# Hybrid attention/LRU layer: attention work placed between the matmul groups of two projections, with a new order of weight tiles

## The reference

```
mod = silu(cond) @ w_mod + b_mod            # 24 blocks of 512 columns: shift, scale, gate twice
h   = rmsnorm(x) * (1 + scale) + shift
u   = h @ w_in                              # 2048 x 5120, split into heads of four mixers
A: differential attention, 4 heads, two softmaxes per head, p0 - lam * p1, then rmsnorm
B: RG-LRU: conv of width 4, gates, scans in both directions, times gelu(gate)   (512 wide)
C: neighbourhood attention, 4 heads, with a bias table
D: grouped attention, 4 query heads, 2 key heads, rms-normed and rotated q and k
y   = concat(A, B, C, D) @ w_out            # 2048 x 2048
x   = x + gate * norm(y)
x   = x + gate2 * norm(swiglu(modulate(norm(x)) @ w_ffn_in) @ w_ffn_out)   # hidden 5632
```

## Time and profile before

| | |
|---|---|
| median of 3 runs | 1934.77 us (1931.64 to 1935.92) |
| profiled execution, its own time | 1931.91 us |
| its span | 1930.1 us |
| PE busy | 1801.7 us, 93% |
| DVE, ACT, POOL busy | 859.8, 653.1, 156.3 us |
| input projection starts at PE | 53.06 us |
| last input matmul to first output-projection matmul group after the turns of A | 513.6 to 641.0 us |
| output projection | 641.0 to about 782.9 us |
| tail to first `up` matmul | to 797.97 us |
| up and down projections | to about 1908 us |

### The profile page before, as it was taken

One profiled execution on the slowest core, in us unless ns is written; L12 is line 12 of the kernel. 1 busy time (PEld: TensorE's weight loads), 2 busy tenths in 40 slices (PEclk: granted clock), 3 DMA queues, 4 the chain that ended last, 5 costly groups with the idle time before them and its releaser, 6 DMA issues.

```text
span 1930.1 us, 22007 instructions
## 1 busy us (share of the span) xinstructions
PE 1801.7 (93%) x9291; PEld 1526.0 (79%) x9291; DVE 859.8 (45%) x1197; ACT 653.1 (34%) x915; POOL 156.3 (8%) x223
## 2 busy tenths in 40 slices
PE   4999979999876899799999999999999999999995
PEld 0666646667555688799999999999999888888884
DVE  4355457722176333743333333333333345555553
ACT  2322234422265233432222222222222234444441
POOL 1000285520010000200000000000000000000000
PEclk9999989999989899899999999999999999999998
DMA  9677755797810333143333333333333333333321
GB/s 374 266 307 300 293 229 217 283 321 302 332 72 1 131 111 129 45 152 131 129 116 127 132 131 129 116 127 131 131 129 116 126 109 131 131 124 119 128 88 66
DMA packets 46298, 315.20 MB, mean 163 GB/s; under 512 B 5388, under 2 KB 7816, under 8 KB 8888
## 3 DMA queue, kind: packets, MB, share of 16 engines
q1 hardware_dynamic: 43328, 298.99, 41.4%
q0 software_dynamic: 2544, 11.59, 1.6%
q10 hardware_dynamic: 328, 3.21, 0.4%
HBM read 308.40 MB, written 5.37 MB: 163 GB/s over the span
## 4 chain that ended last, share of the span: by engine, by line
PE 85%; DVE 5%; POOL 3%; DMA 3%; ACT 2%; issue 1%; DVEq 0%; SPq 0%; ACTq 0%; POOLq 0%
PE ps L867 38%; PE ps L617 8%; PE ps L618 8%; PE ps L619 8%; PE ps L659 5%; PE ps L660 5%; PE ps L661 5%; PE ps L596 3%; DMA raw<-in_weights 2%; DVE wlo L928 1%; POOL pool_t L1322 1%; DVE smalls L1146 1%; DMA ident<-in_ident_c 1%; PE ps L841 1%; PE ps L790 1%
## 5 line engine op out<-in xcount | busy, mean ns | idle before, releaser
L928 DVE TENSOR_TENSOR wlo<-raw,whi 128x1024 fp32r<-128x1024 f32 x376 | 459.7, 1234 | 872.7 <-ACT whi L323 872.5
L323 ACT ACTIVATE whi<-raw 128x1024 fp32r<-128x1024 f32 x376 | 392.8, 1059 | 938.3 <-PE ps L867 505.4
L867 PE MATMUL ps<-h_hi,whi 128*128 128x384 f32 x1408 | 471.3, 335 | 0.1
L867 PE MATMUL ps<-h_hi,wlo 128*128 128x384 f32 x1408 | 470.3, 334 | 0.0
L867 PE MATMUL ps<-h_lo,whi 128*128 128x384 f32 x1408 | 470.3, 334 | 0.0
L867 PEld LDWEIGHTS ps<-h_hi,whi 128*128 128x128 f32 x1408 | 264.3, 188 | 0.2 <-issue 0.2
L867 PEld LDWEIGHTS ps<-h_lo,whi 128*128 128x128 f32 x1408 | 264.3, 188 | 0.0
L867 PEld LDWEIGHTS ps<-h_hi,wlo 128*128 128x128 f32 x1408 | 264.3, 188 | 0.0
L617 PE MATMUL ps<-whi,j_hi 128*128 128x512 f32 x528 | 209.8, 397 | 4.6 <-DVE j_lo L1267 4.6
L659 PE MATMUL ps<-whi,h_hi 128*128 128x512 f32 x480 | 195.6, 407 | 17.7 <-ACT U L350 10.7
L618 PE MATMUL ps<-whi,j_lo 128*128 128x512 f32 x528 | 206.5, 391 | 0.0
(11 more groups left out here) (238 smaller groups left out, 1518.3 us busy)
## 6 DMA issues: line engine op xcount, KB each, us to landing
raw<-in_weights SPq DMA_DIRECT2D x284, 1024.0 KB, 4.9
xT<-in_x_t ACTq DMA_DIRECT2D x1, 3072.0 KB, 13.0
out<-x_sb POOLq DMA_DIRECT2D x3, 1024.0 KB, 4.7
x_sb<-in_x_sample POOLq DMA_DIRECT2D x1, 2048.0 KB, 10.3
gw<-in_lru_gate_w SPq DMA_DIRECT2D x4, 256.0 KB, 2.9
out<-U POOLq DMA_DIRECT2D x4, 256.0 KB, 8.1
nabias<-rpb_pad POOLq DMA_DIRECT2D x16, 64.0 KB, 12.5
x_sb<-in_x_prompt POOLq DMA_DIRECT2D x1, 1024.0 KB, 6.0
```

The source lines that it names most:

```text
L323: nc.scalar.activation(whi[:, 2 * (g % RING) + b], raw[:, t % RAW, HK * b:HK * b + HK].rearrange("p k n -> p (k n)"), ACT.Copy).then_inc(w ...
L867: return nc.tensor.matmul(ps[bank][:, 0:T], w[:, k % KH * P:(k % KH + 1) * P], xs[:, k, :], start=first, stop=last)
L928: V.tensor_tensor(wlo[:, 2 * (t % RAW) + b], raw[:, t % RAW, HK * b:HK * b + HK].rearrange("p k n -> p (k n)"), whi[:, 2 * (g % RING) + b] ...
```

## The change

Attention is cut into tasks and these are set into gaps. Step s now has three gaps, one after each token block's 12 matmuls; gap g = 3s + block. The output projection's 16 tiles become steps 40 to 55. Tasks are K and Q (turn keys, queries), S (scores), P (transpose probabilities), V (value product). A table gives each gap its tasks: D heads from gap 85, A heads from 107, C heads from 131 to 152; 69 gaps hold something, 142 bursts in all. All outputs are now stored row-wise in U and turned back by three transposes per head (`turn_back`), D's in gaps 120 to 123, A's in 138 to 141, C's in 143 to 153. The output projection goes K part by K part (B, D, A, C), each step a sum of its own that ACT copies (first part) or DVE adds to `y1` (`group_add`). Division by the softmax sum moves behind the value product (`evict`). The squares of D's norm move from POOL to ACT (`norm_squares`), the LRU's tanh from `lru_in` into `lru_gates`, the loads of the caches to other places, and the first `in` tile is read as the ninth tile, before the four tiles of row 2 of `mod`. In the tail all three token blocks are done behind the last `group_add`, with the residual add in four pieces of 512.

```
-IN_BLOCKS = [3, 4, 8, 9, 0, 1, 2, 5, 6, 7]
+IN_BLOCKS = [3, 8, 4, 9, 0, 1, 2, 5, 6, 7]
+OUT_KG = [1, 3, 0, 2]
+STEPS = IN_STEPS + OUT_N * KG
+def mod_tiles(s):
+    if s < IN_STEPS:
+        m, first = 2 + s // 2, s % 2 * 2
+        return m, [] if s == 0 else [0, 1, 2, 3] if s == 1 else [first, first + 1]
+    if s - IN_STEPS in (2, 3, 4, 5):
+        m, first = 22 + (s - IN_STEPS - 2) // 2, s % 2 * 2
+        return m, [first, first + 1]
+    return 0, []
```

The places of a head's tasks, from its first gap, for A and for the others:

```
+            s_at, p_at, v_at, q_at, span = (0, 2, 4), (2, 4, 6), (3, 5, 7), 3, 6
...
+            s_at, p_at, v_at, q_at, span = (0, 1, 3), (2, 3, 5), (3, 4, 6), 4, 5
```

PE, behind each token block of a step, and the wait before each turn, since all turns share one bank:

```
+                    if tb == 0 and mid is not None and s >= EARLY * KG:
+                        mod_turn(mid)
+                    gap(TB * s + tb)
...
+            def t_bank(task):
+
+                if T_NO[task]:
+                    pe.wait_ge(t_cp, T_NO[task])
+                else:
+                    pe.wait_ge(l_tanh, 16)
```

ACT, per step:

```
+                if s > EARLY * KG:
+                    gap(s - 1, 2)
+                if KG - 1 in kgs:
+                    rows_out(m)
+                hi(*step_key(s + 1))
...
+                if s >= EARLY * KG:
+                    gap(s, 0)
+                    gap(s, 1)
```

DVE, per step (n is 0 to 3 in the last four steps), and the tail:

```
+                if s > EARLY * KG:
+                    gap(s - 1, 2)
+                if n >= 0:
+                    diagonal(G_M, n, 1, 2 * n)
+                lo(*step_key(s + 1))
+                if n > 0:
+                    for tb in range(TB):
+                        y1_gate(n - 1, tb)
...
+                if s >= EARLY * KG:
+                    gap(s, 0)
+                    if n >= 0:
+                        diagonal(G_M, n, 0, 2 * n + 1)
+                    if KG - 1 in kgs:
+                        mod_out(m)
...
+                if s >= EARLY * KG:
+                    gap(s, 1)
+            gap(STEPS - 1, 2)
             dve.wait_ge(x1_in, 32)
             for tb in range(TB):
+                y1_gate(3, tb)
                 dve.wait_ge(y_g, 9 + tb + 1)
                 dve.wait_ge(rs_done, 2 + tb)
-                V.scalar_tensor_tensor(x_sb[:, tb, :], y1[:, tb, :], yrs[:, tb:tb + 1], x_sb[:, tb, :],
-                                       ALU.mult, ALU.add).then_inc(x1_ok, 1)
+                for n in range(4):
+                    x = x_sb[:, tb, n * NC:n * NC + NC]
+                    ins = V.scalar_tensor_tensor(x, y1[n][:, tb, :], yrs[:, tb:tb + 1], x, ALU.mult, ALU.add)
+                ins.then_inc(x1_ok, 1)
```

POOL (the 16 bias loads follow the load of kvC, as before):

```
+            pool.dma_start(kvD[:, :, :], cgqa.rearrange("b a j p h d -> p (b a j) (h d)")).then_inc(kvd_in, 16)
...
+            pool.wait_ge(l_y, 4)
+            pool.dma_start(kvA[:, :, :], cdiff.rearrange("b a j p h d -> p (b a j) (h d)")).then_inc(kva_in, 16)
...
+            pool.wait_ge(pv_ps, A0)
+            pool.wait_ge(l_xp, 4)
+            pool.wait_ge(stored, stores[0])
             pool.wait_ge(rpb_w, 80)
+            pool.dma_start(kvC[:, :, :], cna.rearrange("b a j p h d -> p (b a j) (h d)")).then_inc(kvc_in, 16)
```

More of the change, by code:

```diff
@@ L66, in tile_plan @@
     for s in range(STEPS):
[L67 to L70, removed]
+        m, kgs = mod_tiles(s)
+        plan += [("mod", m, kg) for kg in kgs] + [step_key(s)]
     plan += [("up", f, part) for f in range(FK) for part in range(2)]
@@ L272, in mod_bank @@
         def mod_bank(m):
[L274 removed]
+            return 7 if m < 8 and m % 2 else 3
         def last_step(n):
@@ new lines, in queries_turn, with scores @@
+            def queries_turn(hd):
+                t_bank(("Q", hd))
+                for tb in range(TB):
+                    ins = nc.tensor.transpose(ps[6][:, tb * P:(tb + 1) * P], q_of(TB * hd + tb), ident[:, :])
+                ins.then_inc(t_ps, 1)
+            def scores(u):
+                kind, h, tb = UNITS[u]
+                hd = u // TB
+                pe.wait_ge(t_cp, T_NO["Q", hd] + 1)
+                if kind == "A" or u == C0:
+                    pe.wait_ge(ex, u)
+                elif u >= 2:
+                    pe.wait_ge(ex, u - 1)
+                for j in range(nsoft(kind)):
+                    part = slice(64 * j, 64 * j + 64) if kind == "A" else slice(0, P)
+                    ins = nc.tensor.matmul(ps[score_bank(u, j)][:, 0:width(tb)], qT[hd % 2][part, tb * P:(tb + 1) * P],
+                                           kT[K_SLOT[hd]][part, keys(tb)], start=True, stop=True)
+                ins.then_inc(sc_ps, 1)
@@ new lines, in gap @@
+            def gap(g):
+                for what, n in GAPS[g]:
+                    if what == "V":
+                        values(n)
+                    elif what == "P":
+                        p_transposes(n)
+                    elif what == "K":
+                        keys_turn(n)
+                    elif what == "Q":
+                        queries_turn(n)
+                    else:
+                        scores(n)
+                if g == TB * IN_STEPS - 1:
+                    pe.wait_ge(l_y, 4)
+                    pe.wait_ge(mod_col, 22)
+                    nc.tensor.transpose(ps[3][0:8, 0:P], stc[:, :], ident[:, :]).then_inc(st_t, 1)
+                if g in CONV:
+                    turn_back(*CONV[g])
+                if g >= TB * (STEPS - OUT_N) and g % TB < 2:
+                    gains(2 * (g // TB - STEPS + OUT_N) + g % TB)
@@ L780, in scores @@
-            def scores(u):
-                kind, h, tb = UNITS[u]
-                hd = u // TB
-                pe.wait_ge(prep_cp, hd + 1)
-                if u >= 2:
-                    pe.wait_ge(ex, u - 1)
-                if u == 0:
-                    pe.wait_ge(st_cp, 1)
-                for j in range(nsoft(kind)):
-                    part = slice(64 * j, 64 * j + 64) if kind == "A" else slice(0, P)
-                    ins = nc.tensor.matmul(ps[2 + 2 * (u % 2) + j][:, 0:width(tb)], qT[hd % 2][part, tb * P:(tb + 1) * P],
-                                           kT[hd % 2][part, keys(tb)], start=True, stop=True)
-                ins.then_inc(sc_ps, 1)
```

768 lines of the change are left out of this document (409 added, 359 removed).

## The result

The changed kernel takes **1866.16 us** (median of 4 runs, 1865.45 to 1866.84), the kernel before 1934.37 us beside it: ratio 0.9649, 95% interval 0.9632 to 0.9666, 68.2 us less.

What follows compares the result with a forecast made beforehand. The prediction took PE to bound both projections, and attention to be a ping-pong of three engines each short of work. Its terms summed to -43.0 us from 1931.9, or 1888.9; with 2.9 us for the median it forecast 1890 us, 1868 to 1912.

Steps and rivals of the forecast that it cites:

- Item 1: Attention between the last input matmul and the output projection: this stretch goes, -127.4 us.
- Items 2 and 3: Attention's PE work inside the steps 58.3 us, other mod rows 9.2, changing between projection and bursts 7 (0 to 14).
- Item 4, waits in the gaps: Attention gaps: PE waits for late weights in A heads 5 us, turns back 2.8, clock loss after last-step waits 2.5.
- waits all hidden: Rival: the schedule's slack covers the new waits, about 1870 us, with free changes 1863; chance 0.12.
- Item 4, last four steps: Last four steps: PE waits for DVE's second diagonal, 2.9 us in three steps, 0.8 in the first, 9.5 us.
- Item 5: LRU rounds: the 10.7 us wait and its slow matmuls go, -12.5 us; wait before gates -2; longer ACT round +1.
- Item 6: Caches: bias loads move to steps 36 and 37 and the late tile's loss moves with them, 0 us (-6 to +3).
- Items 7 and 8: First tile split earlier, less two mod tiles in the way, -0.9 us; tail's residual adds all after last group, +4.5.
- second rival: Rival: small idle gaps keep PE's clock at 0.88 from step 28 to 54, 42 us more, 1932; chance 0.06.
- gap work stuck behind something late: Rival: late weight tiles delay hi and ACT's gap copies in steps 28 to 41, 56 us, 1946; chance 0.05.
- listed signs of being wrong: Clock 0.9 in burst steps, turned-probability waits over 20 us, hi waiting over 5.5 us each input step, or an unnamed wait.
- Another sign: Sign of being right: the first output matmul starts about 60 us earlier.

Runs made afterwards that it cites:

- turns_twice: The changed kernel with every turn of keys and queries done twice, 76 transposes more: 1871.54 us.
- gap_shift: The changed kernel with all attention one gap later, so a 384-key unit of each A head has its scores in a step's last gap: 1866.85 us.
- weights_held: The changed kernel with two idle row reductions on DVE ahead of the weights of A's units of 128 keys: 1870.82 us.
- pool_squares: The changed kernel with the norm's squares and sums back on POOL and both norms in round 0, tanh still behind the gates: 1880.73 us.
- diag_first: The changed kernel with the second diagonal of each of the last four steps ahead of the previous column block's three gates: 1859.33 us.
- bias_pieces: The changed kernel with POOL's one bias add of 2048 columns cut into eight adds of 256: 1864.03 us.
- bias_spread: The changed kernel with the sixteen bias loads issued four at a time, each group one attention unit later, the long add left whole: 1864.04 us.
- all_four: The changed kernel with second diagonal before gates, bias add in eight pieces, block 0's residual earlier, and POOL's LRU polynomial after DVE's convolution: 1854.14 us.
- control: The changed kernel unaltered, timed again: 1866.19 us.

## Why the prediction was wrong, and where it was right

**Item 1, "The stretch of 127.4 us goes": too short by 3.8 us, a second step that failed.** I ended the stretch at 641.0. The output projection's first matmul came only after the turns back and a split, and both went too:

```profile
640.83 2.77 PE L832 MATMUL ps<-ident,U 128*128 128x128 f32 x12
...
644.77 0.50 PE L617 MATMUL ps<-whi,h_hi 128*128 128x512 f32 x1 [1.17 <-DVE h_lo L1197]
```

The new turns were charged (0.33 a head), the old ones not credited. A slip in reading the trace before, not a surprise of the chip.

**Items 2 and 3, the PE work and the changes (58.3 + 9.2 + 7): right.** From step 28 to the last output matmul the changed kernel takes 346.7 us with that matmul. Less 28 steps of 8.19 (229.3), 15 pairs of mod tiles (30.8), 8 turns of mod (3.9), 8 spreads (6.9), the waits on the diagonal (5.1) and step 37's 3.1 and 1.3, that leaves 66.3 us for twelve heads and 69 gaps; 65.3 were forecast. Only the sum is measured: if the heads take their 58.3 us, changing over costs 0.12 us a gap, not 0.1. turns_twice bears out the price of a transpose (0.10 us, 0.11 in the sum).

**Item 4, waits in the gaps (5 + 2.8 us, and 2.5 for the clock): the step that failed.** None came; 10.3 us too much. I took the unit whose scores stand in the last gap of a step for one of 384 keys, with maxima and exps behind hi and lo. (The 8.2 us that I gave for it is not even the sum of its terms, 4.6 + 2.0 + 2.4 = 9.0.) It has 128 keys, since A heads begin at gaps 107, 113, 119 and 125 with their short unit, and DVE and ACT run its maxima and exps ahead of hi and lo, as their code has it. ACT around the start of step 42 (550.88), the exp at once, then the tile:

```profile
550.04 0.37 ACT L547 ACTIVATE pb<-ps,smalls 128x128 f32<-128x128 f32 x1 [0.35 <-DVE smalls L1242]
...
553.13 2.01 ACT L407 ACTIVATE whi<-raw 128x1024 fp32r<-128x1024 f32 x2 [2.28 <-DMA raw<-in_weights]
```

Only the weights stay behind lo, and DVE ends them just as PE asks:

```profile
557.20 0.35 DVE L1257 SCALAR_TENSOR_TENSOR pb<-pb,smalls,pb 128x128 f32<-128x128 f32 x1
```

```profile
557.61 0.33 PE L903 MATMUL ps<-ident,pb 128*128 128x128 f32 x1
```

gap_shift shows that even the larger unit costs 0.7 us there, once in four heads, and weights_held that this cover is not to be spent. With this the rival "waits all hidden" was the nearer story (its 17 us left out the 2.8 for the turns back; with them it stands at 1870). At 0.12 it had too small a chance: I had put a price on each possible lateness without walking one unit through its three queues.

**Item 4, last four steps (9.5 us): mechanism right, size not.** Three waits of 1.71, none in step 52, 5.1 us. Lo ended 5.0 us after the step began, not 5.6, and a gate follows a gate after 0.60 us, not 0.69: instructions of DVE that stand in a row overlap by a tenth of a microsecond, which I had allowed only the diagonals. A wait of 1.7 us cost no clock: the stretch shows 1.00.

**Item 5 (-13.5): measured -16.0, in one of the quickest executions.** Executions of the changed kernel whose LRU was not edited give -11.6 to -16.0, and the forecast lies among them. The 10.7 us wait went with its slow matmuls, as said, and pool_squares gives it back at 14.8. Before the gate matmuls PE waits 0.59 us instead of 2.30, and they take 2.85 us instead of 4.54; I had counted the wait and not the slowness behind it. Where the wait came back at 3.25 to 3.50 us (diag_first, bias_pieces, bias_spread), they took 4.30 to 4.54 again. I blamed DVE's scans, and the trace before does not bear that out. DVE was through with them and idle for 0.93 us; ACT had waited 4.56 us for the weight tile, and the convolution then ran at its full pace, 2.45 us (ACT, then DVE):

```profile
265.49 2.01 ACT L323 ACTIVATE whi<-raw 128x1024 fp32r<-128x1024 f32 x2 [4.56 <-DMA raw<-in_weights]
```

```profile
266.59 2.38 DVE L928 TENSOR_TENSOR wlo<-raw,whi 128x1024 fp32r<-128x1024 f32 x2 [0.93 <-ACT whi L323]
268.89 0.47 DVE L1045 TENSOR_SCALAR lru_xc<-lru_xp,pc 128x388 f32<-128x388 f32 x1
269.40 1.94 DVE L1048 SCALAR_TENSOR_TENSOR lru_xc<-lru_xp,pc,lru_xc 128x388 f32<-128x388 f32 x3
```

POOL's polynomial beside the convolution is a cost of the changed kernel in this round, 1.3 us, which all_four takes away.

**Item 6 (0): right by luck.** Steps 28 to 39 held 6 us of such loss before and hold 4.5 now. But the cause now is the add behind the loads, not the loads landing together (0.8 us at most). In the trace before, the add (530.71, 4.52 us) ran beside row maxima from PSUM, which took their usual 0.29 and 0.56 us; DVE's next instruction with two inputs in SBUF came at 535.38, when it had ended.

**Items 7 and 8 (-0.9, +4.5): -1.2 and +3.8.** Right, item 7 within a scatter of 2 to 3 us in the early steps.

**Rivals and signs.** The clock stayed at 1.00 in every stretch with bursts but steps 37 (0.93) and 38 (0.97), behind the one long wait. The swing that the second rival feared did not occur, and outside step 37 PE does not stand between bursts and projection at all. Hi's waits for its tile were 0.9 to 4.5 us. The one case of gap work stuck behind something late, step 37, came from POOL. It is one of the listed signs of being wrong, a wait that no item names. Another sign was off as well: the first output matmul came at 525.28 instead of 644.77, 119 us earlier and not 60, since half of attention's gaps now lie behind it; the sum doesn't rest on that.

Sum of the miss from step 28 on: 3.8 (item 1) + 10.3 - 1 (items 2 to 4) + 4.4 (last steps) + 1.7 (item 6) = 19.2 of 19.7 us.

## What to carry to other kernels

Work of a stage that several engines play back and forth was worth hardly more than its bare PE time here, once it was cut into pieces between long runs of matmuls. Whether its hand-overs are hidden is settled by walking one unit through each engine's queue in written order, not by adding up durations. When a stretch is taken out, end it at the first instruction of the next stage. Before placing a long POOL instruction, look what short DVE instructions with both inputs in SBUF fall beside it, and cut it up or put it where they have slack.

## What the runs showed of the hardware

- POOL's add of 2048 columns (4.56 us) held DVE's add of 8 columns from 490.57 to 494.75, 4.18 us instead of 0.17; moved, it held an instruction of one column for 3.21 us instead of 0.22; in weights_held it held the low parts of a tile for 6.76 us instead of 2.36. Cut in eight, the longest hold seen beside it was about 0.6 us (1.17 against 0.62). By the Trainium skill, SBUF — State Buffer (SBUF: two separate sides), the port pair that the two engines share is an exclusive lock for a whole instruction, and a DVE instruction with two SBUF inputs needs it against a POOL instruction that reads SBUF. The ends, 494.75 and 494.72, agree, and so do the row maxima from PSUM before the change, which the same add left at their usual length.
- The same at small size: in round 1 of the LRU a convolution that takes 2.45 us alone (kernel before, all_four) takes 3.7 us beside POOL's polynomial, ahead of PE's gate matmuls. It takes these 3.7 us in every execution of the changed kernel in which that POOL work runs beside it, quick or slow, so it is no cause of the 4 us of scatter. The scatter goes for the most part with the landing of a weight tile. Where ACT's hi waited 0.36 us for it (changed kernel), PE waited 0.59 before the gate matmuls; 0.57 gave 1.28 (control), 1.86 gave 2.27 (weights_held), 2.79 gave 3.50 (diag_first). Why the tile lands later in some executions is not shown.
